# An expert stage in which a product of 512 columns replaces two of 256, and VectorE adds the halves

## The chip, the cores and the metric

The kernel runs on one core of one Trainium2 chip. The metric is its time on the device in microseconds (us), the median of several executions.

## The reference, cut to what matters

A network of two blocks and a third, for 256 tokens of width 1024 in float32. All of it runs in one kernel; the change lies in the last part, a feed-forward layer of 16384 small experts, of which each token picks a few. The kernel computes it densely:

```
act[e, t]   = gelu(sum_d w_down[e, d] * h[t, d])      for all 16384 experts e
out[t, :]  += sum_e gate[e, t] * act[e, t] * w_up[e, :]
```

`gate[e, t]` is zero for nearly all pairs. It is a sum over the picks of token t, each an outer product of two one-hot vectors of length 128 with a weight.

## The kernel before, in words

Each 32-bit weight w is split into a high part, `whi` (w rounded to fp32r), and a low part, `wlo` = w - `whi`; activations likewise (`hhi`, `hlo`, `chi`, `clo`). A product is then three: high x high, high x low and low x high. `pe_mm3` (lines 556 to 573) issues the three.

**Blocks.** SyncE loads slabs of 2048 columns into a ring of 3 (`raw`). A slab is two blocks of 1024 columns. ScalarE makes the high part of a block (line 2400, `cut_hi`), then VectorE or GpSimd the low part (line 1345, `cut_lo`), both into rings of 3 blocks. ScalarE waits until TensorE has used up the block three before. Which engine makes a low part is said by `lo_engine`: in the two earlier feed-forward layers VectorE and GpSimd take turns, of the expert layer's first 12 blocks GpSimd makes all, and VectorE all that follow. `ve_cuts` and `se_cuts` let each engine run two blocks ahead of the block that TensorE is at.

**The expert layer.** The 16384 experts are 128 groups of 128, called "experts" 0 to 127 in the code and here. Expert i has a down block (8 tiles of 128x128) and an up block (1024 columns). Its down block gives `h` times `w_down`, 128 experts x 256 tokens, in one half of a PSUM bank (24 products of 256 columns, `pe_expert_down`); ScalarE applies gelu from PSUM (line 2945); VectorE multiplies with the gates (line 2347), rounds (2352) and subtracts (2354), `ve_weigh`; then 12 products of 512 columns with the up block add into four banks that hold the output (lines 565 to 567).

The order has four stretches:

- down blocks 0 to 20, while VectorE picks the experts of each token;
- down blocks 21 to 71, "where gates are built": between them stand 64 gate steps, one or two behind each of the experts 21 to 68 (`steps`). For a step VectorE makes one-hots for four tokens (four TENSOR_SCALAR, line 2324, and one TENSOR_TENSOR of 512 columns, line 2327), TensorE multiplies them (line 1300), ScalarE copies the result out (line 2959), and DMAs spill it. Results of gelu wait in `ge_t`;
- up blocks 0 to 70 alone;
- from expert 72 (`NST`) on, down and up blocks alternate: down i+1, up i.

PSUM banks go round: all eight where gates are built, four for the down blocks behind.

All is written by hand: each engine has its own list of work (`pe_`, `ve_`, `se_`, `ge_`, and `sync` for the DMAs), and semaphores are counted from it.

## Time and profile before

| | |
|---|---|
| runs | 1988.35 us median of 3 (1988.26 to 1988.54) |
| profiled execution, its own time | 1988.46 us |
| its span, first to last instruction | 1986.7 us |
| TensorE (PE) busy | 1897.9 us, 96% |
| VectorE (DVE) busy | 1384.1 us, 70% |
| ScalarE (ACT) busy | 990.0 us, 50% |
| GpSimd (POOL) busy | 257.1 us, 13% |
| mean granted TensorE clock | 0.989 |

PEld is TensorE's load of weights, which runs beside its products. Busy times are averages over stretches with different limits, so a stretch is read by itself. A product is pipelined: its duration overlaps the next one, and the distance from start to start is its price. The same holds in small for VectorE and ScalarE: an instruction that waits for nothing starts some 0.09 us before the end of the one ahead.

### The profile page before, as it was taken

To read this page: it belongs to the slowest core of one execution; us is meant where nothing else is said; L and a number is where in the kernel's file an instruction comes from. 1 tells how busy PE (TensorE), PEld (TensorE's weight loads), DVE (VectorE), ACT (ScalarE), POOL (GpSimd) and SP (SyncE) were. 2 spreads that over 40 slices of the span, in tenths; PEclk is the share of its full clock that TensorE was granted. 3 is DMA by queue.
4 is the path that set the end of the run, shared out by engine and by line. 5 is a ranking of instruction groups with operands and counts; after the bars stand their busy time and mean duration, and the time that the engine had idled before them with its cause. 6 is when DMAs were issued, how large, how long until landed. Compare 5 with 4: busy or idle time off the path is not lost.

```text
span 1986.7 us, 33458 instructions
## 1 busy us (share of the span) xinstructions
PE 1897.9 (96%) x13306; PEld 1751.9 (88%) x13306; DVE 1384.1 (70%) x2518; ACT 990.0 (50%) x1442; POOL 257.1 (13%) x118
## 2 busy tenths in 40 slices
PE   6989899999988999999999899999999999999998
PEld 6887799999968799999898799999988888999997
DVE  5897775558957773347666559988878887666665
ACT  5645544455435554455555445566653334444444
POOL 0001044440001034430000065000000000000000
PEclk8999999999999999999999999999999999999999
DMA  8754467765564255545434354577766866465452
GB/s 319 245 189 142 150 237 258 258 225 199 183 229 154 97 194 181 188 170 201 166 129 168 111 175 161 184 219 215 219 206 255 301 240 231 179 231 193 174 208 107
DMA packets 94553, 391.96 MB, mean 197 GB/s; under 512 B 7680, under 2 KB 41776, under 8 KB 56000
## 3 DMA queue, kind: packets, MB, share of 16 engines
q1 hardware_dynamic: 94112, 389.58, 56.4%
q8 instruction: 106, 1.74, 0.4%
q14 instruction: 47, 0.39, 0.1%
q10 hardware_dynamic: 288, 0.26, 0.1%
HBM read 371.72 MB, written 15.73 MB: 195 GB/s over the span
## 4 chain that ended last, share of the span: by engine, by line
PE 77%; DVE 11%; ACT 3%; issue 2%; DMA 1%; POOL 0%; ACTq 0%; DVEq 0%; SPq 0%
PE ps L569 10%; PE ps L571 10%; PE ps L570 10%; PE acc L565 9%; PE acc L566 9%; PE acc L567 9%; PE acc L569 3%; PE acc L570 3%; PE acc L571 3%; DVE wlo L1345 2%; PE ps L1300 1%; PE acc L1300 1%; DVE arena L1374 1%; PE ps L1043 1%; PE ps L714 1%
## 5 line engine op out<-in xcount | busy, mean ns | idle before, releaser
L2400 ACT ACTIVATE whi<-raw 128x1024 fp32r<-128x1024 f32 x557 | 588.7, 1060 | 484.7 <-PE acc L567 273.1
L1345 DVE TENSOR_TENSOR wlo<-raw,whi 128x1024 fp32r<-128x1024 f32 x461 | 569.2, 1242 | 292.6 <-ACT whi L2400 289.5
L569 PE MATMUL ps<-hhi,whi 128*128 128x256 f32 x1848 | 527.3, 285 | 7.0 <-DVE wlo L1345 3.1
L571 PE MATMUL ps<-hhi,wlo 128*128 128x256 f32 x1848 | 522.8, 283 | 0.0
L570 PE MATMUL ps<-hlo,whi 128*128 128x256 f32 x1848 | 522.7, 283 | 0.0
L569 PEld LDWEIGHTS ps<-hhi,whi 128*128 128x128 f32 x1848 | 354.1, 192 | 12.9 <-issue 4.1
L570 PEld LDWEIGHTS ps<-hlo,whi 128*128 128x128 f32 x1848 | 354.3, 192 | 2.8
L571 PEld LDWEIGHTS ps<-hhi,wlo 128*128 128x128 f32 x1848 | 354.1, 192 | 0.0
L1345 POOL TENSOR_TENSOR wlo<-raw,whi 128x1024 fp32r<-128x1024 f32 x96 | 239.8, 2501 | 616.6 <-ACT whi L2400 616.4
L565 PE MATMUL acc<-whi,chi 128*128 128x512 f32 x752 | 296.0, 394 | 3.5 <-DVE wlo L1345 1.9
L566 PE MATMUL acc<-whi,clo 128*128 128x512 f32 x752 | 294.5, 392 | 0.0
L567 PE MATMUL acc<-wlo,chi 128*128 128x512 f32 x752 | 293.5, 390 | 0.0
L569 PE MATMUL acc<-hhi,whi 128*128 128x256 f32 x672 | 195.3, 291 | 11.5 <-DVE wlo L1345 4.8
L570 PE MATMUL acc<-hlo,whi 128*128 128x256 f32 x672 | 191.1, 284 | 0.0
L571 PE MATMUL acc<-hhi,wlo 128*128 128x256 f32 x672 | 191.1, 284 | 0.0
L565 PEld LDWEIGHTS acc<-whi,chi 128*128 128x128 f32 x752 | 142.1, 189 | 32.5 <-issue 2.9
L567 PEld LDWEIGHTS acc<-wlo,chi 128*128 128x128 f32 x752 | 141.8, 189 | 30.4
L566 PEld LDWEIGHTS acc<-whi,clo 128*128 128x128 f32 x752 | 142.1, 189 | 26.3
L1374 DVE SCALAR_TENSOR_TENSOR arena<-arena,gs_t 128x512 f32<-128x512 f32 x140 | 130.9, 935 | 24.5 <-DMA arena<-in_ada 15.4
L569 PEld LDWEIGHTS acc<-hhi,whi 128*128 128x128 f32 x672 | 129.9, 193 | 14.5 <-ACT hhi L2514 4.6
L570 PEld LDWEIGHTS acc<-hlo,whi 128*128 128x128 f32 x672 | 130.1, 194 | 0.0
L571 PEld LDWEIGHTS acc<-hhi,wlo 128*128 128x128 f32 x672 | 129.9, 193 | 0.0
(452 smaller groups left out, 2399.7 us busy)
## 6 DMA issues: line engine op xcount, KB each, us to landing
raw<-in_peer_down SPq DMA_DIRECT2D x64, 1024.0 KB, 5.0
raw<-in_peer_up SPq DMA_DIRECT2D x64, 1024.0 KB, 5.0
arena<-in_ada SPq DMA_DIRECT2D x80, 512.0 KB, 5.1
raw<-in_w_gate SPq DMA_DIRECT2D x22, 1024.0 KB, 4.8
raw<-in_w_up SPq DMA_DIRECT2D x22, 1024.0 KB, 4.8
raw<-in_w_down SPq DMA_DIRECT2D x22, 1024.0 KB, 4.8
arena<-spill SPq DMA_DIRECT2D x14, 1024.0 KB, 7.0
spill<-hT_t SPq DMA_DIRECT2D x22, 448.0 KB, 5.9
```

Of the source, the lines that this page charges most:

```text
L565: e.matmul(out, xh, hi, start=start, stop=False, skip_group_check=True)
L566: e.matmul(out, xl, hi, start=False, stop=False, skip_group_check=True)
L567: i = e.matmul(out, xh, lo, start=False, stop=stop, skip_group_check=True)
L569: e.matmul(out, hi, xh, start=start, stop=False, skip_group_check=True)
L570: e.matmul(out, hi, xl, start=False, stop=False, skip_group_check=True)
L571: i = e.matmul(out, lo, xh, start=False, stop=stop, skip_group_check=True)
L714: i = e.matmul(ps[:, j * 128:(j + 1) * 128], self.m.ada_acc[:, j * 128:(j + 1) * 128], self.m.ones, start=True, stop=True, skip_group_chec ...
L1043: t = e.matmul(ps[0:30, 0:256], m.zb[:, 8 * i + k, :], w[:, k, :], start=i == 0 and k == 0, stop=i == 1 and k == 7, skip_group_check=True)
L1300: t = e.matmul(ps[:, i * 128:(i + 1) * 128], m.oh1[:, n % 3, i * 128:(i + 1) * 128], m.oh2[n % 3][:, i * 128:(i + 1) * 128], start=True, s ...
L1345: e.tensor_tensor(out=lo, in0=w, in1=hi.bitcast(F32), op=ALU.subtract).then_inc(*X(("lo", j)))
L1374: e.scalar_tensor_tensor(out=m.ada_acc, in0=w, scalar=c, in1=m.ada_acc, op0=ALU.mult, op1=ALU.add).then_inc(*V(*([("ada", s)] if k else [])))
L2400: e.activation(hi, w, ACT.Copy, scale=1.0).then_inc(*self.A(("hi", j)))
```

## The change

- `hhi` and `hlo` become the halves of one buffer, `hpair`, so that one operand (`hP`) can take the high and the low activations of a tile side by side, 2 x 256 columns.
- From expert 21 (`STEP0`) on a tile of a down block is two products (`pe_mm2`): high weights x 512 columns into the whole bank, and low weights x the 256 high columns into its first half.
- VectorE adds the two halves of the bank with a TENSOR_REDUCE (`ve_halves`) into `ge_t` or `co`; gelu (`se_gelu`) then works in place on SBUF. Experts 0 to 20 keep the old way.
- `lo_engine`: of the down blocks 21 to 71 the second of each slab (experts 21, 23, ... 71) goes to GpSimd.
- Where gates are built, ScalarE copies out the gates of expert i-1's steps and applies its gelu one block later, behind the high part that it cuts for expert i.

```diff
@@ lo_engine
+        if name == "peer_down" and STEP0 <= 2 * i + half < NST:
+            return ("V", "G")[half]
@@ Memory
-        hhi, hlo = sb("hhi", [128, 2048], F32R), sb("hlo", [128, 2048], F32R)
+        hpair = sb("hpair", [128, 4096], F32R)
...
+        self.hP = hpair[:, :].rearrange("p (s a t) -> p a s t", s=2, a=8)
+        self.hH, self.hL, self.cH, self.cL = self.hP[:, :, 0, :], self.hP[:, :, 1, :], tiles8(chi), tiles8(clo)
@@ new
+    def pe_mm2(self, e, ps, tile, k, *keys):
+        hi, lo, end = tile
+        if end is not None:
+            keys = (*keys, ("used", end))
+        e.matmul(ps.rearrange("p (s t) -> p s t", s=2), hi, self.m.hP[:, k], start=k == 0, stop=False, skip_group_check=True)
+        i = e.matmul(ps[:, 0:T], lo, self.m.hH[:, k, :], start=False, stop=k == 7, skip_group_check=True)
...
+    def ve_halves(self, e, dst, *key):
+        src = self.banks.tile(*key)[:, :].rearrange("p (s t) -> p t s", s=2)
+        e.wait_ge(*self.at("full", *key))
+        e.tensor_reduce(out=dst, in_=src, axis=AX, op=ALU.add, negate=False).then_inc(*self.V(("out", *key)))
@@ ve_gates
             self.ve_cuts(e, "peer_down", 8 * i + 7)
+            if i > STEP0:
+                self.ve_expert_halves(e, i - 1)
@@ ve_experts
         self.ve_weigh(e, 0)
+        self.ve_expert_halves(e, NST - 1)
         for i in range(128):
             if i + 1 >= NST and i < 127:
                 self.ve_cuts(e, "peer_down", 8 * (i + 2) - 1)
+            if NST <= i + 1 < 128:
+                self.ve_expert_halves(e, i + 1)
+                self.ve_cuts(e, "peer_up", 8 * (i + 1) - 1)
             if i < 127:
                 self.ve_weigh(e, i + 1)
@@ se_gates
+            self.se_cuts(e, "peer_down", 8 * i + 7)
+            if i > STEP0:
+                for n in steps(i - 1):
+                    self.se_gates_out(e, n)
+                self.se_gelu(e, i - 1)
@@ se_experts
             if i + 1 >= NST and i < 127:
-                self.se_expert_down(e, i + 1)
+                self.se_cuts(e, "peer_down", 8 * (i + 1) + 7)
+                if i + 1 == NST:
+                    self.se_gelu(e, NST - 1)
+                self.se_gelu(e, i + 1)
```

The order of instructions at two places. First VectorE where gates are built; L1345 (before) and L1363 (after) make a low part, the rows with `kc_t` are one-hots (one gate step is a row of L2324 and one of L2327), L1400 adds halves. Before, three experts:

```order
L1345 TENSOR_TENSOR wlo<-raw,whi 128x1024
L2324 TENSOR_SCALAR arena<-kc_t,arena 128x128 x4
L2327 TENSOR_TENSOR arena<-kc_t,arena 128x512
L1345 TENSOR_TENSOR wlo<-raw,whi 128x1024
L2324 TENSOR_SCALAR arena<-kc_t,arena 128x128 x4
L2327 TENSOR_TENSOR rs_t<-kc_t,arena 128x512
L1345 TENSOR_TENSOR wlo<-raw,whi 128x1024
L2324 TENSOR_SCALAR arena<-kc_t,arena 128x128 x4
L2327 TENSOR_TENSOR rs_t<-kc_t,arena 128x512
```

After the change, three experts:

```order
L2351 TENSOR_SCALAR arena<-kc_t,arena 128x128 x4
L2354 TENSOR_TENSOR rs_t<-kc_t,arena 128x512
L1400 TENSOR_REDUCE arena<-acc 128x256
L2351 TENSOR_SCALAR arena<-kc_t,arena 128x128 x4
L2354 TENSOR_TENSOR rs_t<-kc_t,arena 128x512
L2351 TENSOR_SCALAR arena<-kc_t,arena 128x128 x4
L2354 TENSOR_TENSOR arena<-kc_t,arena 128x512
L1363 TENSOR_TENSOR wlo<-raw,whi 128x1024
L1400 TENSOR_REDUCE arena<-ps 128x256
L2351 TENSOR_SCALAR arena<-kc_t,arena 128x128 x4
L2354 TENSOR_TENSOR rs_t<-kc_t,arena 128x512
L1400 TENSOR_REDUCE arena<-ps 128x256
```

What moved: behind each expert's one-hots there is a reduction, and only one expert in two has a low part left on VectorE. The other 26 stand on POOL, in the order of their blocks: it has 88 low parts behind the first feed-forward layer's 34, where it had 62.

Second, VectorE where down and up blocks alternate. One pair before (`x2`: an up block and the next down block):

```order
L2354 TENSOR_TENSOR clo<-rs_t,chi 128x256
L1345 TENSOR_TENSOR wlo<-raw,whi 128x1024 x2
L2347 TENSOR_TENSOR rs_t<-rs_t,arena 128x256
L2352 CAST chi<-rs_t 128x256
L2354 TENSOR_TENSOR clo<-rs_t,chi 128x256
```

and after:

```order
L2388 TENSOR_TENSOR clo<-rs_t,chi 128x256
L1363 TENSOR_TENSOR wlo<-raw,whi 128x1024
L1400 TENSOR_REDUCE rs_t<-ps 128x256
L1363 TENSOR_TENSOR wlo<-raw,whi 128x1024
L2381 TENSOR_TENSOR rs_t<-rs_t,arena 128x256
L2386 CAST chi<-rs_t 128x256
L2388 TENSOR_TENSOR clo<-rs_t,chi 128x256
```

What moved: the two low parts are torn apart. Behind the one of the down block stands the reduction, then the low part of the up block, and then the weighing (`rs_t`, CAST, `clo`), which stood ahead of it. On ACT the order is as before, gelu and then two high parts, but gelu now waits for the reduction.

## Rows read from the trace of the kernel before

**Rows 1.** The page: the span, and the busy time of PE.
```profile
span 1986.7 us, 33458 instructions
...
PE 1897.9 (96%) x13306; PEld 1751.9 (88%) x13306; DVE 1384.1 (70%) x2518; ACT 990.0 (50%) x1442; POOL 257.1 (13%) x118
```

**Rows 2.** Busy time per stretch: start:end, its length, each engine (instructions), clock, DMA share, GB/s.
```profile
1264.00:1460.00 196.00, 196.00 (x1672) 195.97 (x1671) 160.97 (x365) 131.22 (x161) 0.00 (x0) 1.00 0.72 213
...
1470.00:1660.00 190.00, 190.00 (x840) 157.39 (x839) 159.28 (x279) 74.27 (x70) 0.00 (x0) 1.00 0.69 249
...
1664.00:1960.00 296.00, 296.00 (x1898) 270.10 (x1897) 184.90 (x265) 126.24 (x158) 0.00 (x0) 1.00 0.54 200
```

**Rows 3.** Order of time, PE, one pair: start us, duration us, engine, line, operation.
```profile
1812.05 0.28 PE L569 MATMUL ps<-hhi,whi 128*128 128x256 f32 x1
...
1814.92 0.40 PE L565 MATMUL acc<-whi,chi 128*128 128x512 f32 x1
...
1817.67 0.28 PE L569 MATMUL ps<-hhi,whi 128*128 128x256 f32 x1
```

**Rows 4.** The same view, PE, where gates are built: the first product of two down blocks.
```profile
1383.42 0.37 PE L569 MATMUL acc<-hhi,whi 128*128 128x256 f32 x1
...
1395.62 0.37 PE L569 MATMUL acc<-hhi,whi 128*128 128x256 f32 x1
```

**Rows 5.** The same view, DVE, where gates are built.
```profile
1380.09 1.11 DVE L2324 TENSOR_SCALAR arena<-kc_t,arena 128x128 f32<-128x128 f32 x4
...
1381.12 0.68 DVE L2327 TENSOR_TENSOR rs_t<-kc_t,arena 128x512 f32<-128x512 f32 x1
...
1381.72 1.22 DVE L1345 TENSOR_TENSOR wlo<-raw,whi 128x1024 fp32r<-128x1024 f32 x1
...
1382.85 1.11 DVE L2324 TENSOR_SCALAR arena<-kc_t,arena 128x128 f32<-128x128 f32 x4
...
1385.82 1.23 DVE L1345 TENSOR_TENSOR wlo<-raw,whi 128x1024 fp32r<-128x1024 f32 x1 [1.25 <-ACT whi L2400]
```

**Rows 6.** The same view, DVE and POOL in the first FFN; then the view of line 1371.
```profile
262.45 1.54 DVE L1374 SCALAR_TENSOR_TENSOR arena<-arena,gs_t 128x512 f32<-128x512 f32 x2
...
265.23 3.50 DVE L1374 SCALAR_TENSOR_TENSOR arena<-arena,gs_t 128x512 f32<-128x512 f32 x2
...
264.16 3.23 POOL L1345 TENSOR_TENSOR wlo<-raw,whi 128x1024 fp32r<-128x1024 f32 x1 [3.00 <-ACT whi L2400]
...
L1371 DVE TENSOR_SCALAR arena<-arena,gs_t x20: 444/478/2573, 45.7 to 707.3; 128x512 f32<-128x512 f32 x20
```

**Rows 7.** Groups of DVE instructions by line and shape: busy us, mean ns.
```profile
L2324 DVE TENSOR_SCALAR arena<-kc_t,arena 128x128 f32<-128x128 f32 x256 | 71.1, 341 | 0.0
...
L1553 DVE TENSOR_REDUCE small<-arena 128x2 f32<-128x512 f32 x20 | 13.7, 686 | 0.7
...
L1575 DVE COPY arena<-ps 128x512 f32<-128x512 f32 x12 | 7.9, 687 | 6.1 <-PE ps L744 5.8
...
L1567 DVE TENSOR_SCALAR arena<-arena,small 128x256 f32<-128x256 f32 x40 | 12.3, 351 | 0.7
```

**Rows 8.** Order of time, DVE and ACT, one pair.
```profile
1815.54 0.43 DVE L2347 TENSOR_TENSOR rs_t<-rs_t,arena 128x256 f32<-128x256 f32 x1 [0.91 <-ACT rs_t L2945]
...
1816.67 1.22 DVE L1345 TENSOR_TENSOR wlo<-raw,whi 128x1024 fp32r<-128x1024 f32 x1
...
1815.12 0.38 ACT L2945 ACTIVATE rs_t<-ps 128x256 f32<-128x256 f32 x1 [1.75 <-PE ps L571]
...
1815.40 1.05 ACT L2400 ACTIVATE whi<-raw 128x1024 fp32r<-128x1024 f32 x1
```

**Rows 9.** The same view, PE, from the last down product of the gates' stretch.
```profile
1465.26 0.28 PE L571 MATMUL ps<-hhi,wlo 128*128 128x256 f32 x1
...
1467.10 0.47 PE L565 MATMUL acc<-whi,chi 128*128 128x512 f32 x1 [1.56 <-DVE clo L2354]
```

More of the change, by code:

```diff
@@ L300, in tiles8 @@
             return ap[:, :].rearrange("p (a t) -> p a t", a=8)
-        self.hH, self.hL, self.cH, self.cL = tiles8(hhi), tiles8(hlo), tiles8(chi), tiles8(clo)
+        self.hP = hpair[:, :].rearrange("p (s a t) -> p a s t", s=2, a=8)
+        self.hH, self.hL, self.cH, self.cL = self.hP[:, :, 0, :], self.hP[:, :, 1, :], tiles8(chi), tiles8(clo)
         self.hT = tiles8(self.hT_t)
@@ L571, in pe_mm3 @@
             i = e.matmul(out, lo, xh, start=False, stop=stop, skip_group_check=True)
+        if keys:
+            i.then_inc(*self.P(*keys))
+    def pe_mm2(self, e, ps, tile, k, *keys):
[4 more added lines that the diff above has]
+        i = e.matmul(ps[:, 0:T], lo, self.m.hH[:, k, :], start=False, stop=k == 7, skip_group_check=True)
         if keys:
@@ L1268, in pe_expert_down @@
         ps = self.banks.take(e, "expert", i)
+        if i >= STEP0:
+            for k in range(8):
+                self.pe_mm2(e, ps, self.W.tile(e, "peer_down", 8 * i + k), k, *([("full", "expert", i)] if k == 7 else []))
+            return
         for k in range(8):
@@ L2329, in ve_one_hots, with ve_expert_halves @@
                             *V(("oh2", n)))
+    def ve_expert_halves(self, e, i):
+        m = self.m
+        if i >= NST + 2:
+            e.wait_ge(*self.at("weighed", i - 2))
+        self.ve_halves(e, m.ge_t[i] if i < NST else m.co[:, i % 2, :], "expert", i)
     def ve_weigh(self, e, i):
@@ L2336, in ve_weigh @@
         w = m.co[:, 2 + s, :]
-        e.wait_ge(*self.at("out", "expert", i))
+        e.wait_ge(*self.at("gelu", i))
         if i == 0:
@@ L2940, in se_expert_down, with se_gelu, se_gates_out @@
         e.wait_ge(*self.at("full", "expert", i))
-        if i >= NST + 2:
-            e.wait_ge(*self.at("weighed", i - 2))
-        elif i == NPRE + 16:
-            e.wait_ge(*self.at("end", "picked", "P"))
-        e.activation(m.ge_t[i] if i < NST else m.co[:, i % 2, :], self.banks.tile("expert", i)[:, 0:T],
-                     ACT.Gelu_apprx_tanh, scale=1.0).then_inc(*self.A(("out", "expert", i)))
+        e.activation(m.ge_t[i], self.banks.tile("expert", i)[:, 0:T], ACT.Gelu_apprx_tanh, scale=1.0).then_inc(
+            *self.A(("out", "expert", i), ("gelu", i)))
+    def se_gelu(self, e, i):
+        x = self.m.ge_t[i] if i < NST else self.m.co[:, i % 2, :]
+        e.wait_ge(*self.at("out", "expert", i))
+        e.activation(x, x, ACT.Gelu_apprx_tanh, scale=1.0).then_inc(*self.A(("gelu", i)))
     def se_gates(self, e):
-        m, A = self.m, self.A
         for i in range(STEP0, NST):
-            self.se_expert_down(e, i)
-            for n in steps(i):
-                k, c = n // 2 % 3, n // 6
-                st = m.stage[k].rearrange("p (n t) -> p n t", t=8)[:, :, 4 * (n % 2):4 * (n % 2) + 4]
-                e.wait_ge(*self.at("full", "gates", n))
-                if c and n % 2 == 0:
-                    e.wait_ge(self.spilled[k], 16 * c)
-                    e.wait_ge(self.kept, 16 * (n // 2 - 2))
-                e.activation(st.rearrange("p n t -> p t n"), self.banks.tile("gates", n)[:, :].rearrange(
-                    "p (t n) -> p t n", t=4), ACT.Copy, scale=1.0).then_inc(*A(("out", "gates", n)))
+            self.se_cuts(e, "peer_down", 8 * i + 7)
[3 more added lines that the diff above has]
+                self.se_gelu(e, i - 1)
+    def se_gates_out(self, e, n):
+        m = self.m
+        k, c = n // 2 % 3, n // 6
+        st = m.stage[k].rearrange("p (n t) -> p n t", t=8)[:, :, 4 * (n % 2):4 * (n % 2) + 4]
+        e.wait_ge(*self.at("full", "gates", n))
+        if c and n % 2 == 0:
+            e.wait_ge(self.spilled[k], 16 * c)
+            e.wait_ge(self.kept, 16 * (n // 2 - 2))
+        e.activation(st.rearrange("p n t -> p t n"), self.banks.tile("gates", n)[:, :].rearrange("p (t n) -> p t n", t=4),
+                     ACT.Copy, scale=1.0).then_inc(*self.A(("out", "gates", n)))
     def se_experts(self, e):
```

## The prediction

> The time for a change is worked out against the profiled execution: span 1986.7 us, its own time 1988.46 us, which is 0.1 us over the median of the runs shown, 1988.35. What the change adds to or takes from the span is added to that median. About 0.2%, 4 us, is what a measurement of this kernel can tell from no change.
>
> **What bounds the kernel now.** First the page: PE is busy 1897.9 of 1986.7 us [rows 1]. Then the stretches that the change touches, taken alone: where gates are built (1264 to 1460), where up products run alone (1470 to 1660) and where down and up products alternate (1664 to 1960), PE is busy for all of 196, 190 and 296 us, at a granted clock of 1.00, while DVE is busy for 161, 159 and 185 [rows 2]. Busy time does not say at which pace, so the next view is the order of time on PE. In the alternating stretch a down block, 24 products of 256 columns, takes 1812.05 to 1814.92, 0.1196 us each, and an up block, 12 products of 512 columns, 1814.92 to 1817.67, 0.229 us each; then the next down block follows with no gap [rows 3]. The durations of 0.28 and 0.40 in these rows overlap each other; the steps from start to start are what counts. Where gates are built, three experts with their four gate steps take 1383.42 to 1395.62, 12.20 us [rows 4]. So PE alone sets both paces: 12.20 us for three experts, and 2.87 + 2.75 = 5.62 us for a pair of blocks.
>
> **1. Products of 512 columns.** A tile now costs 0.229 + 0.120 = 0.349 us where it was 3 x 0.1196 = 0.359. The same columns stream; only one start is saved. Per expert 8 x 0.010 = 0.08 us, 2.79 where it was 2.87. For 107 experts (21 to 127) that is 8.6 us at most: 4.1 in the 51 experts of the gates' stretch, 4.5 in the 56 behind. The moving operand is now two pieces of 256 columns, which no row shows. The bounds are one product of 512 (0.229) and two of 256 (0.239, which would give nothing back); I take the first. One weight load less changes nothing, since loads lie beside products.
>
> **2. The halves added on DVE.** 107 new TENSOR_REDUCE from 512 elements in PSUM to 256. Nearest rows: a reduce from 128x512 takes 686 ns, a COPY of 512 from PSUM 687 [rows 7], so I take 0.69 us, or 0.60 from start to start behind another (a 0.68 us one-hot product is followed after 0.60 [rows 5]). None of the rows has 256 outputs; from below one of 0.60, from above two passes, 1.3. Gelu moves behind it and reads SBUF: 0.38 us from PSUM [rows 8], at most 0.05 more.
>
> The Trainium skill (VectorE: DVE Perf Modes, the TRN2 errata) counts 62 cycles more for a PSUM source than for SBUF. That would be 0.75 us here and a total of +11, an estimate from that page; the equal 686 and 687 speak against it.
>
> **3. Half the low parts to GpSimd.** 26 blocks (experts 21, 23 to 71) leave DVE, 1.13 us each from start to start [rows 5], and cost GpSimd some 2.4. GpSimd is otherwise empty there, and PE needs a block two experts after the one whose buffer it takes is used, some 8.1 us [rows 4]; that covers 1.06 + 2.4. What is not covered is DVE. In the trace DVE stands still while GpSimd subtracts: two SCALAR_TENSOR_TENSOR take 1.54 us with GpSimd idle and 3.50 while GpSimd runs from 264.16 to 267.39, which is itself stretched to 3.23 by DVE's subtraction before [rows 6]. That is 1.96 us lost per GpSimd operation. A TENSOR_SCALAR of 128x512 whose median is 478 ns took up to 2573 [rows 6], so one-input operations from SBUF are caught too. It runs at double pace: from 256 columns (351 ns [rows 7]) to 512 it needs 0.127 us more, where one column per clock from PSUM needs 0.69 for 512. The one-hots of L2324 are of that kind (341 ns with two scalars) and will be caught. Operations from PSUM, which no row shows beside GpSimd, I take to be free of it.
>
> By the Trainium skill (SBUF, Who interferes with whom) the pair of ports is an exclusive lock, taken by operations with two SBUF inputs and by fast one-input modes, never by tensor_reduce. The trace agrees, by rows 6, for the first two.
>
> **4. The sum where gates are built**, per six experts (eight gate steps, three low parts on each engine). PE: 24.40 before, 24.40 - 6 x 0.08 = 23.92 now. DVE: a step is 1.03 + 0.60 = 1.63 [rows 5], eight are 13.04; three low parts 3.39; six reductions 3.60; together 20.03, about what it was (13.04 + 6.78 = 19.82). To this come three stalls. Full stalls of 2.03 (1.96 and a little wait for the handover) less a reduction running under each would be 1.43; the middle, 1.73, gives 5.19. Sum 25.2. DVE then sets the pace, 0.8 over the old 24.40. Over the 48 experts with steps: 8 x 0.82 = **+6.6 us**. Who waits: PE's gate steps, for one-hots. Bounds: all stalls hidden, PE at 23.92, -4; three whole operations of 2.4, 27.2, +22.
>
> **5. End of the gates' stretch.** Before, PE pauses from the last down product at 1465.26 to 1467.10, for DVE's first weighing [rows 9]. Now DVE has halves of expert 70 and its backlog in front of it: 0.6 to 1.2, **+1 us** taken.
>
> **6. First pair.** Gelu of expert 71 stands on ACT behind the high part of down block 73, which waits until PE has used up block 70. From there 1.05 + 0.4 (gelu) + 1.13 (weighing) + 1.2 (low part of up block 71) with hand-overs is 4.0 us, against 2.79 of down block 72: **+1.2**, and some 0.6 until the chain has settled: **+1.8**.
>
> **7. The alternating stretch.** PE now needs 2.79 + 2.75 = 5.54 us for a pair. DVE and ACT form a ring: halves (0.69), gelu (0.28 to 0.33 until the next ACT start), high part 1.05, low part of the up block 1.13, weighing 1.13 (1815.54 to 1816.67), low part of the down block 1.13, next halves; with two hand-overs of 0.03 to 0.04 that is 5.48 to 5.53 [rows 5, 7, 8]. Before, the low part of the up block stood behind the weighing and nothing closed the ring. It is as long as PE's own 5.54, so PE keeps the pace by a hair: 56 x 0.08 = **-4.5 us**. Each 0.1 us more in the reduction would cost 5.6.
>
> The 71 up blocks alone are unchanged. SP's order is unchanged too: slabs wait for the same low parts, and three ring slots cover a GpSimd block's 1.3 us more. The wait for the bank (now freed by DVE) has eight banks behind it. Sum: 6.6 + 1.0 + 1.8 - 4.5 = +4.9, so 1993.3 us.
>
> **Rivals.**
> A, *the stalls are hidden and PE keeps both paces*. For it: DVE was idle for 35 of 196 us [rows 2], and a GpSimd block may fall on waits and reductions. It decides if a GpSimd operation costs DVE under (23.92 - 20.03) / 3 = 1.3 us. Then -4.1 + 0.5 + 1.8 - 4.5 = -6.3: 1982.0. Against it: DVE's idle time came from waits for high parts in front of low parts, and these are the halves that GpSimd now makes.
> B, *the reduction is dearer*, since it writes 256 results, or the split moving operand gives nothing. At 0.9 us DVE's ring is 5.72, +0.10 x 56 = +5.6 in place of -4.5; the gates' stretch gets 8 x 6 x 0.2 = +9.6 more: +24.6, 2013. At 0.75: some 1998.
> C, *whole GpSimd operations fall on DVE*: 2.4 each, +22 in place of +6.6: 2009.
> That halves or GpSimd blocks are not there is excluded by the order of the instructions.
>
> **Chances.** Forecast 0.50 (+1 to +12; of it 0.14 within 4 us), A 0.23 (nearly all below -4, 0.03 within), B 0.16, C 0.11. Faster 0.20, same 0.17, slower 0.63. The range leaves out the dearest of B and the far end of A: 1980 to 2009.
>
> **What would show it.** In the gates' stretch DVE near 100% busy, with one-hots of over 2 us beside each GpSimd low part; PE no longer full, waiting for DVE's one-hots; about 202 us for what took 196. The new reduction at 0.69. Down blocks of 2.79 on PE. In the alternating stretch a period of 5.54 to 5.56, and DVE's halves starting right behind its low part. I am wrong if PE stays full where gates are built (A), if the reduction is over 0.8 us or a 512-column product over 0.235 (B).

## The result, and the profile after

The changed kernel takes **1998.3 us** (median of 6 runs, 1995.91 to 2004.54), the kernel before on the same chips 1987.8 us (6 runs). The ratio is 1.0061, 95% interval 1.0048 to 1.0073: slower by 10.5 us as a difference of the medians, by 12 as the ratio has it. 1993.3 us was forecast, a change of +4.9. The direction is right and the main cause is right; the change came out 5.6 us dearer.

The profiled execution of the changed kernel took 2004.54 us, 6 us over its median. 3.7 us of its distance to the profile before arise ahead of everything that the change touches (the last COPY_PREDICATED of the expert choice starts at 1257.63 where it was 1253.94); the granted clock from 600 to 660 us was 0.89 there and 0.95 in the profile before, and 0.91 against 1.00 from 900 to 920. What follows therefore goes by the length of stages, not by the span.

The page of the changed kernel: span, busy time, and the chain that ended last by engine and by line.

```profile
span 2002.7 us, 31852 instructions
...
PE 1899.2 (95%) x12450; PEld 1709.7 (85%) x12450; DVE 1455.8 (73%) x2599; ACT 992.5 (50%) x1442; POOL 319.9 (16%) x144
...
PE 68%; DVE 21%; ACT 3%; issue 2%; DMA 1%; POOL 0%; ACTq 0%; DVEq 0%; SPq 0%
```

PE is as busy as before [rows 1] although it has fewer products, and DVE now has 21% of the chain, where it had 11%. The windows of the changed kernel (start:end, length, then PE, PEld, DVE, ACT, POOL busy, clock, DMA share, GB/s): first to last gate step, six microseconds just behind the first up product, and the stretch in which down and up blocks alternate.

```profile
1273.20:1470.60 197.40, 190.60 (x1263) 172.59 (x1264) 197.40 (x387) 127.09 (x155) 55.47 (x23) 1.00 0.67 204
1482.00:1488.00 6.00, 6.00 (x21) 4.73 (x20) 4.22 (x8) 1.06 (x1) 0.00 (x0) 0.72 0.28 119
1664.00:1960.00 296.00, 294.81 (x1469) 247.15 (x1468) 212.98 (x318) 127.04 (x157) 0.00 (x0) 1.00 0.52 199
```

Against [rows 2]: where gates are built DVE is busy for all of 197.40 us and PE no longer is. Before, the same piece of work, first to last gate step, was this window, 192.4 us long, with PE full and DVE at 159.8:

```profile
1264.20:1456.60 192.40, 192.40 (x1641) 192.39 (x1640) 159.79 (x363) 128.66 (x158) 0.00 (x0) 1.00 0.71 211
```

The reason stands in the order of time of DVE where gates are built, changed kernel.

```profile
1378.58 3.22 DVE L2351 TENSOR_SCALAR arena<-kc_t,arena 128x128 f32<-128x128 f32 x4
1381.72 0.68 DVE L2354 TENSOR_TENSOR arena<-kc_t,arena 128x512 f32<-128x512 f32 x1
1382.33 0.68 DVE L1400 TENSOR_REDUCE arena<-ps 128x256 f32<-128x512 f32 x1
1382.93 1.10 DVE L2351 TENSOR_SCALAR arena<-kc_t,arena 128x128 f32<-128x128 f32 x4
...
1387.91 0.68 DVE L1400 TENSOR_REDUCE arena<-ps 128x256 f32<-128x512 f32 x1
1388.52 2.60 DVE L2351 TENSOR_SCALAR arena<-kc_t,arena 128x128 f32<-128x128 f32 x4
```

The same for GpSimd.

```profile
1378.56 2.40 POOL L1363 TENSOR_TENSOR wlo<-raw,whi 128x1024 fp32r<-128x1024 f32 x1 [4.71 <-ACT whi L2438]
1387.84 2.42 POOL L1363 TENSOR_TENSOR wlo<-raw,whi 128x1024 fp32r<-128x1024 f32 x1 [6.89 <-ACT whi L2438]
```

Four one-hots take 1.10 us with GpSimd idle, and 3.22 where its subtraction starts with them. At 1387.84 it starts 0.07 us ahead of a reduction; the reduction takes its usual 0.68 us and only the one-hots behind it are held, 2.60 us. Of the 24 GpSimd blocks that meet one-hots, 15 begin ahead of a reduction like this one and hold the one-hots for 1.5 us; the other nine hold them for 1.9 to 2.2. Over the whole stretch the mean of a one-hot rose from 341 ns [rows 7] to 496:

```profile
L2351 DVE TENSOR_SCALAR arena<-kc_t,arena 128x128 f32<-128x128 f32 x256 | 111.8, 496 | 0.0
```

The 256 of them took 111.8 us where they took 71.1 [rows 7]. That is 1.7 us for each of the 24; of the other two GpSimd blocks, one runs beside the expert choice and one behind the last gate step.

The reduction itself: the view of its line in the changed kernel (ns as min/median/max), and who waited for it.

```profile
L1400 DVE TENSOR_REDUCE rs_t<-ps x56: 682/684/693, 1681.4 to 1988.8; 128x256 f32<-128x512 f32 x56
L1400 DVE TENSOR_REDUCE arena<-ps x27: 671/680/684, 1275.8 to 1481.2; 128x256 f32<-128x512 f32 x27
...
  ACT rs_t L2986: 142.3, 56
```

Two stalls stand at the start of the gates' stretch. PE's waits from 1250 to 1480 in the changed kernel (total us, times, longest):

```profile
PE ps L1318 <- DVE rs_t L2354: 4.6, 4, 1.8
PE acc L572 <- DVE wlo L1363: 3.4, 3, 2.5
PE acc L1318 <- DVE arena L2354: 1.8, 2, 0.9
PE acc L1318 <- DVE rs_t L2354: 1.3, 2, 0.9
PE ps L1318 <- DVE arena L2354: 0.8, 1, 0.8
```

Before, the longest wait for a low part in this place was 0.6 us. What DVE did there, changed kernel; GpSimd's first two blocks run from 1258.61 and from 1269.26:

```profile
1257.63 4.51 DVE L2277 COPY_PREDICATED arena<-arena 128x256 f32<-128x256 uint32 x2
...
1269.52 2.99 DVE L2351 TENSOR_SCALAR arena<-kc_t,arena 128x128 f32<-128x128 f32 x4
```

The two COPY_PREDICATED took 2.61 us before. DVE's next low part is 1.9 us later for it, and PE waits for that. The first one-hots are held as well, so from the last of the picked transposes (six products that turn the picked experts' numbers round for the gate steps) to the first gate step it is 4.9 us instead of 3.0.

Last, PE in the alternating stretch of the changed kernel: the first pair's stall, and later one down block from its first product to that of the up block, and the next down block.

```profile
1680.52 0.47 PE L568 MATMUL acc<-whi,chi 128*128 128x512 f32 x1 [1.18 <-DVE wlo L1363]
...
1683.36 0.39 PE L584 MATMUL ps<-hpair,whi 128*128 128x512 f32 x1
1683.59 0.28 PE L585 MATMUL ps<-hpair,wlo 128*128 128x256 f32 x1
...
1686.17 0.40 PE L568 MATMUL acc<-whi,chi 128*128 128x512 f32 x1
...
1688.96 0.39 PE L584 MATMUL ps<-hpair,whi 128*128 128x512 f32 x1
```

Down block 2.81 us, up block 2.79: a period of 5.60 us, where it was 5.62 [rows 3] and 5.54 was forecast.

The pace where gates are built is best read over equal pieces of work. Eight gate steps and six experts took 24.40 us before [rows 4]. In the changed kernel, from one gate step to the one 24 steps later, PE takes 75.32 us, 25.11 for eight:

```profile
1322.92 1.05 PE L1318 MATMUL acc<-rs_t,arena 128*128 128x128 f32 x8
...
1398.24 1.05 PE L1318 MATMUL ps<-rs_t,arena 128*128 128x128 f32 x8
```

Table of stages, each measured on PE in the profiled execution (us), from start to start. "To first step" runs from the last of the picked transposes to the first gate step; "gate steps" from there to the last product of the last step, which takes in all 64 steps and the 47 down blocks between them; "to up" from the first product of the last step to the first up product; "pairs" from the first down product of expert 72 to the last `whi`, `chi` product of expert 127.

| kernel | to first step | gate steps | to up | 71 up blocks | pairs |
|---|---|---|---|---|---|
| before | 3.0 | 192.4 | 11.25 | 193.2 | 317.7 |
| changed | 4.9 | 197.4 | 11.7 | 194.8 | 317.9 |
| all low parts on DVE | 3.0 | 188.7 | 11.5 | 193.2 | 317.8 |
| GpSimd blocks alone | 5.0 | 193.9 | 11.25 | 193.2 | 317.7 |
| GpSimd blocks cut short | 3.0 | 188.7 | 11.5 | 193.2 | 318.0 |
| halves side by side | 5.0 | 197.8 | 11.7 | 194.9 | 317.9 |
| all on DVE, other orders | 3.0 | 188.7 | 11.5 | 193.2 | 316.2 |
| pairs only | 3.0 | 192.4 | 11.25 | 193.2 | 316.2 |
| GpSimd from expert 27 | 3.0 | 197.4 | 11.7 | 193.2 | 317.9 |
| no halves among pairs | 3.0 | 188.7 | 11.5 | 193.2 | 317.6 |
| 512 first, then 256 | 3.0 | 188.8 | 11.5 | 194.9 | 311.9 |
| a fourth on GpSimd | 3.0 | 192.1 | 11.6 | 193.2 | 317.8 |

### The profile page after: what moved, and what is told of

Same layout as the page of the kernel before. It is cut to its first block, busy times and chain, and to the rows that moved or that the text cites. A ratio compares the mean times of both kernels' runs of the same rounds, so it can differ in the third digit from the quotient of the medians.

```text
span 2002.7 us, 31852 instructions
## 1 busy us (share of the span) xinstructions
PE 1899.2 (95%) x12450; PEld 1709.7 (85%) x12450; DVE 1455.8 (73%) x2599; ACT 992.5 (50%) x1442; POOL 319.9 (16%) x144
## 4 chain that ended last, share of the span: by engine, by line
PE 68%; DVE 21%; ACT 3%; issue 2%; DMA 1%; POOL 0%; ACTq 0%; DVEq 0%; SPq 0%
PE acc L568 9%; PE acc L570 9%; PE acc L569 9%; PE ps L572 6%; PE ps L574 6%; PE ps L573 6%; PE ps L584 5%; DVE arena L2351 5%; DVE wlo L1363 3%; PE ps L585 3%; PE acc L572 2%; PE acc L573 2%; PE acc L574 2%; DVE arena L1400 1%; DVE arena L1392 1%
## 5 line engine op out<-in xcount | busy, mean ns | idle before, releaser
L1363 DVE TENSOR_TENSOR wlo<-raw,whi 128x1024 fp32r<-128x1024 f32 x435 | 537.1, 1242 | 280.1 <-ACT whi L2438 279.6
L1363 POOL TENSOR_TENSOR wlo<-raw,whi 128x1024 fp32r<-128x1024 f32 x122 | 302.5, 2482 | 800.4 <-ACT whi L2438 800.2
L572 PE MATMUL ps<-hpair,whi 128*128 128x256 f32 x1184 | 337.7, 285 | 7.0 <-DVE wlo L1363 3.1
L573 PE MATMUL ps<-hpair,whi 128*128 128x256 f32 x1184 | 335.0, 283 | 0.0
L574 PE MATMUL ps<-hpair,wlo 128*128 128x256 f32 x1184 | 334.9, 283 | 0.0
L584 PE MATMUL ps<-hpair,whi 128*128 128x512 f32 x664 | 238.8, 400 | 0.0
L572 PEld LDWEIGHTS ps<-hpair,whi 128*128 128x128 f32 x1184 | 226.9, 192 | 10.8 <-issue 4.1
L573 PEld LDWEIGHTS ps<-hpair,whi 128*128 128x128 f32 x1184 | 227.1, 192 | 0.6
L574 PEld LDWEIGHTS ps<-hpair,wlo 128*128 128x128 f32 x1184 | 227.0, 192 | 0.0
L585 PE MATMUL ps<-hpair,wlo 128*128 128x256 f32 x664 | 186.1, 280 | 0.0
L572 PE MATMUL acc<-hpair,whi 128*128 128x256 f32 x480 | 140.3, 292 | 15.0 <-DVE wlo L1363 8.3
L584 PEld LDWEIGHTS ps<-hpair,whi 128*128 128x128 f32 x664 | 124.8, 188 | 28.7
L573 PE MATMUL acc<-hpair,whi 128*128 128x256 f32 x480 | 138.2, 288 | 0.0
L574 PE MATMUL acc<-hpair,wlo 128*128 128x256 f32 x480 | 138.1, 288 | 0.0
```

Source lines behind the costliest of these rows:

```text
L572: e.matmul(out, hi, xh, start=start, stop=False, skip_group_check=True)
L573: e.matmul(out, hi, xl, start=False, stop=False, skip_group_check=True)
L574: i = e.matmul(out, lo, xh, start=False, stop=stop, skip_group_check=True)
L584: e.matmul(ps.rearrange("p (s t) -> p s t", s=2), hi, self.m.hP[:, k], start=k == 0, stop=False, skip_group_check=True)
L585: i = e.matmul(ps[:, 0:T], lo, self.m.hH[:, k, :], start=False, stop=k == 7, skip_group_check=True)
L1363: e.tensor_tensor(out=lo, in0=w, in1=hi.bitcast(F32), op=ALU.subtract).then_inc(*X(("lo", j)))
```

## The experiments

My theory after reading the two traces: GpSimd's subtraction holds up DVE instructions beside it, DVE becomes the bound where gates are built, and that costs more than the 512-column products earn. The rivals: the reductions do it, or the later gates, or the memory layout of the moving operand.

### All low parts on DVE

```
         if name[:6] in ("w_gate", "w_up0", "w_up1", "w_down"):
             return ("V", "G")[j % 2]
-        if name == "peer_down" and STEP0 <= 2 * i + half < NST:
-            return ("V", "G")[half]
```

> The changed kernel without the two lines in lo_engine: VectorE makes all low parts where gates are built, GpSimd none. My theory (VectorE loses about 2 us under each of the 26 GpSimd operations): VectorE's own work per six experts rises from 20.0 to 13.04 + 6 x 1.13 + 6 x 0.60 = 23.4 us, but nothing stalls it, and PE needs 24.40 - 6 x 0.06 = 24.0 with the down block of 2.81 us measured after the change. So PE sets the pace again: from the first to the last gate step 185 to 187 us (187.8 before, 196.6 after the change), and a total of 1985 to 1989. Rival (the reductions overload VectorE, whoever makes the low parts): with 3.4 us more of its own per six experts the stretch is as long as after the change or longer, 196 to 203, and the total 1998 to 2006.

Measured: 1980.97 us, ratio to before 0.9976 (0.9964 to 0.9987): **faster than before**, by 0.24%. The window of its gate steps:

```profile
1259.80:1448.50 188.70, 188.70 (x1267) 172.03 (x1265) 186.10 (x410) 132.92 (x157) 0.00 (x0) 1.00 0.70 215
```

PE is full again and DVE, which now makes 23 low parts more in this stretch, is busy for 11 us less than in the changed kernel: each GpSimd block had cost DVE (197.4 - 186.1) / 23 = 0.49 us more than it took off. The work handed to GpSimd was worth more on DVE than off it. The gates' stretch is 3.7 us shorter than before, and both stalls at its start are gone. Without its GpSimd blocks the change would have been a gain. PE's own pace, 24 gate steps apart, is 71.80 us, 23.93 for eight:

```profile
1307.74 1.05 PE L1316 MATMUL acc<-rs_t,arena 128*128 128x128 f32 x8
...
1379.54 1.05 PE L1316 MATMUL ps<-rs_t,arena 128*128 128x128 f32 x8
```

The whole came out 4 us under the lower end of what I had put down; on these chips the kernel before took 1984.8 us, 3 less than on those of the result. The 187.8 and 196.6 us in the expectation were counted from other borders than the table's 192.4 and 197.4.

### GpSimd blocks alone

The kernel before with the two lines of `lo_engine` added and nothing else.

```
+        if name == "peer_down" and STEP0 <= 2 * i + half < NST:
+            return ("V", "G")[half]
```

> The kernel before with only the two lines in lo_engine added: GpSimd makes 26 low parts, products and gelu as before. My theory: each GpSimd operation stalls VectorE by 1.7 to 2.0 us, but VectorE has 13.04 + 3.39 + 3 x 1.9 = 22.1 us per six experts against PE's 24.4, so PE keeps the pace: 187.8 to 189 us from the first to the last gate step, total 1988 to 1990. VectorE's busy time in the stretch rises all the same, from 161 us in 196 to about 175. Rival (PE waits for low parts that GpSimd makes late): the stretch is 190 to 197 us, and PE's waits name POOL's low part.

Measured: 1994.72 us, ratio 1.0039 (1.0023 to 1.0054). The window of its gate steps:

```profile
1270.50:1464.40 193.90, 193.90 (x1641) 193.90 (x1641) 162.28 (x339) 128.52 (x157) 65.49 (x23) 0.99 0.70 209
```

The two COPY_PREDICATED in its order of DVE:

```profile
1254.80 4.50 DVE L2254 COPY_PREDICATED arena<-arena 128x256 f32<-128x256 uint32 x2
```

Here DVE has no reductions, so it has room: 162.28 of 193.90 us, and PE is never without work. The steps cost 1.5 us more than before, and all of that lies in the first eight of them (26.0 us for 24.5; each eight behind take 24.41 as before). There the granted clock was 0.50 for a while, behind PE's waits at the start:

```profile
1272.00:1275.00 3.00, 3.00 (x16) 3.00 (x15) 1.33 (x3) 1.65 (x2) 0.00 (x0) 0.50 0.38 158
```

So in the even part of the stretch GpSimd's blocks cost this kernel nothing. The two stalls at the start are the same as in the changed kernel, 4.50 for 2.61 and 5.0 for 3.0. So they belong to GpSimd's first blocks alone. The whole came out over what I had put down, as I had counted the steps and not the start. DVE's busy time had been expected at about 175 us in 196 and stayed at 162: only 16 of the 26 blocks held one-hots.

### GpSimd blocks cut short

The changed kernel, but GpSimd's operation covers 64 of 1024 columns. The other 960 low parts of those blocks are left out of the result.

```
                 e.wait_ge(*self.at("hi", j))
+                if who == "G" and self.W.blocks[j][0] == "peer_down" and STEP0 <= 2 * self.W.blocks[j][1] + self.W.blocks[j][2]:
+                    w, hi, lo = w[:, 0:64], hi[:, 0:64], lo[:, 0:64]
```

> The changed kernel with the 26 operations of GpSimd cut from 1024 to 64 columns (of these low parts 960 of 1024 columns are left out, so what TensorE reads there is old); VectorE's instructions, their order and every wait are the same. My theory: with some 0.3 us in place of 2.4 per operation VectorE's stalls nearly vanish, and its own 20.0 us per six experts lie far under PE's 24.0: 185 to 186 us from the first to the last gate step, total 1985 to 1989. Rival (the work or the order of the reductions sets the pace): 196 us as after the change, total 1998, since none of that is touched.

Measured: 1982.87 us, ratio 0.9989 (0.9978 to 1.0000).

```profile
1262.30:1451.00 188.70, 188.70 (x1265) 171.99 (x1264) 161.58 (x387) 133.27 (x158) 8.99 (x24) 1.00 0.67 213
```

Order, waits and counts of instructions are those of the changed kernel; only the time in which GpSimd works is taken away, 55 us to 9. DVE falls from 197.4 to 161.6 us and PE is full. What slowed DVE is the overlap itself, not the waits that come with another engine. The steps took 188.7 us where 185 to 186 had been put down, by the other borders named above, and the whole came out 2 us under its range.

### Halves side by side

The high and low halves of one k stand next to each other in memory, so a 512-column product reads 512 words in a row instead of two pieces of 256.

```
-        self.hP = hpair[:, :].rearrange("p (s a t) -> p a s t", s=2, a=8)
+        self.hP = hpair[:, :].rearrange("p (a s t) -> p a s t", s=2, a=8)
```

> The changed kernel with hpair laid out by tiles, so that the 512 columns of the moving operand lie together (2 KB) and not in two pieces 8 KB apart. Theory a (the split operand costs 0.006 us per product, 0.235 from start to start where 0.229 was measured before): down blocks of 2.77 to 2.79 us in place of 2.81, pairs of 5.56 to 5.57, total 1 to 2 us less than the changed kernel. Theory b (the pitch comes from the alternation of 512 and 256 columns, not from the operand): 2.81 and 5.595 as after the change, total unchanged at 1998.

Measured: 1999.63 us, ratio 1.0058 (1.0042 to 1.0073); pairs 317.9 us. No stage differs from the changed kernel by more than 0.4 us, and the 0.4 is in the gate steps, where this execution had a second stretch at a granted clock of 0.50 (1279 to 1282). The split operand is not what makes a down block 2.81 us.

### All on DVE, weighing first, gelu of expert 71 earlier

```
                 self.ve_expert_halves(e, i + 1)
-                self.ve_cuts(e, "peer_up", 8 * (i + 1) - 1)
             if i < 127:
                 self.ve_weigh(e, i + 1)
...
                 self.se_gelu(e, i - 1)
+        self.se_gelu(e, NST - 1)
...
                 self.se_cuts(e, "peer_down", 8 * (i + 1) + 7)
-                if i + 1 == NST:
-                    self.se_gelu(e, NST - 1)
```

and the two lines of `lo_engine` taken out.

> The change without its GpSimd blocks (all low parts on DVE), and two orders altered: DVE weighs an expert right behind its halves, with the low part of the up block after the weighing instead of before it, and ACT does the gelu of expert 71 at the end of the gates' loop, ahead of the high part of down block 73. Theory A (a ring of DVE and ACT sets the pairs' period of 5.60 us: halves, gelu, high part of the up block, its low part, weighing, low part of the down block, halves, all back to back in the trace): the new order opens the ring, so the pairs' period falls to PE's own, 5.54 us or less, and the pairs' stage takes 313 to 315 us instead of 317.83; the stall of 1.2 us behind the first down block of the pairs is gone as well. Whole: about 1977 us beside 1981 for the version with all low parts on DVE, ratio to before 0.995 to 0.997. Theory B (PE's own pitch of 0.232 to 0.235 us for the products beside 512-column ones sets 5.60): the stage falls only by the 1.2 us of the first stall, to 316.6 us, and the whole is about 1979.8 us, ratio 0.997. The gates' steps take 188.7 us either way.

Measured: 1981.07 us, ratio 0.9968 (0.9955 to 0.9981), pairs 316.17 us. The order of DVE in one of its pairs:

```profile
1864.26 1.23 DVE L1361 TENSOR_TENSOR wlo<-raw,whi 128x1024 fp32r<-128x1024 f32 x1 [0.35 <-ACT whi L2435]
1865.99 0.69 DVE L1398 TENSOR_REDUCE rs_t<-ps 128x256 f32<-128x512 f32 x1 [0.50 <-PE ps L583]
```

The ring is open, for DVE now waits 0.50 us for PE ahead of each reduction. Yet the period is 5.60 us, as it was. Theory A falls: DVE and ACT did not set it. The 1.66 us that the stage lost are the stall of the first pair. The whole fits theory B (ratio 0.997), not A.

### Pairs only

The kernel before with `pe_mm2` and the halves from expert 72 on; gates' stretch as before, no GpSimd blocks, gelu of expert 71 from PSUM in its old place.

```
-        if i >= STEP0:
+        if i >= NST:
             for k in range(8):
```

> The kernel before, with the products of 512 columns and the halves from expert 72 on only (gates' stretch as before, no GpSimd low parts). Both theories: the gates' steps take 192.4 us as before and the 71 up blocks 193.2 us. Pairs' stage 317.8 us as in the change (317.66 before), since either the ring or the pitch holds it; so the whole is the time of before, ratio 0.999 to 1.001: the 512-column products earn nothing among the pairs, and the 3.8 us that the all-DVE version gained all come from the gates' stretch. If the ratio were below 0.998, that would be wrong.

Measured: 1986.68 us, ratio 0.9994 (0.9985 to 1.0003), no difference. Its pairs take 316.17 us, 1.6 less than I had put down: there is no first stall, and 512-column products in this order earn 1.5 us over 56 pairs. DVE's order within a pair is that of the changed kernel here, so the old place of expert 71's gelu is enough to take the first stall away.

### GpSimd from expert 27 on

```
-        if name == "peer_down" and STEP0 <= 2 * i + half < NST:
+        if name == "peer_down" and STEP0 + 6 <= 2 * i + half < NST:
```

> The change with GpSimd's low parts from expert 27 on instead of from 21 (23 blocks instead of 26). Theory: the two stalls at the start of the gates' stretch (low part behind the slowed COPY_PREDICATED, +1.9 us; first one-hots, +2.1 us) belong to the first blocks on GpSimd and go: the wait of PE for the last low part of the route is 0.6 us again, and from the last picked transpose to the first gate step 3.6 us instead of 5.7. The gates' steps keep most of their 197.4 us, since DVE is still caught by the others: about 196.5 us (three blocks of 26 fewer, 8.7 us times 3/26 = 1 us less). Whole about 5 us under the change: 1993 us beside 1998, ratio to before 1.003 to 1.004. Rival: the two stalls come from the products of 512 columns or from the later gates, and stay; then the whole is within 1.5 us of the change, ratio 1.005 to 1.006.

Measured: 1993.41 us, ratio 1.0039 (1.0025 to 1.0053). Both stalls at the start are gone: the longest wait for a low part of the expert choice is 0.6 us, and the first gate step comes 3.0 us behind the picked transposes (the expectation's 3.6 and 5.7 count from an earlier product). Its interval is clear of the one with all low parts on DVE, so the rest of the loss is still there:

```profile
1261.90:1459.30 197.40, 190.30 (x1264) 172.44 (x1264) 197.40 (x389) 128.13 (x156) 53.04 (x22) 1.00 0.67 205
```

The steps take 197.4 us where I expected 196.5. I had counted three blocks fewer, but two of the three start ahead of the first gate step: the window holds 22 in place of 23. At 0.49 a block, 22 give 186.1 + 10.8 = 196.9; that even this half microsecond does not show stays open. The whole is 0.22% under the changed kernel. The two intervals overlap a little, but the vanished stalls stand in the trace, so some 4 us of the loss arise at the start of the stretch and the rest inside it.

### A fourth of the low parts on GpSimd

```
-        if name == "peer_down" and STEP0 <= 2 * i + half < NST:
-            return ("V", "G")[half]
+        if name == "peer_down" and STEP0 + 6 <= 2 * i + half < NST:
+            return ("V", "G")[half * (i % 2)]
```

> The change with GpSimd making only every fourth down block's low part from expert 27 on: 12 blocks instead of 26. Theory (each GpSimd block takes 1.22 us of its own off DVE and adds some 1.7 us to the DVE instructions beside it, so it costs DVE 0.47 us, and the gates' steps take the larger of PE's 188.7 us and DVE's 186.1 + 0.47 a block): DVE's sum is 186.1 + 12 x 0.47 = 191.7 us, steps 190.5 to 192.5 us, no stalls at the start, whole some 3 us over the version with all on DVE, ratio to before 0.998 to 1.000. Rival (one block in four finds cover, since DVE has 2.6 us free in the steps and PE has a queue ahead): steps 188.7 us, ratio 0.997.

Measured: 1985.91 us, ratio 1.0000 (0.9988 to 1.0012).

```profile
1260.10:1452.20 192.10, 189.60 (x1266) 172.31 (x1265) 192.10 (x400) 130.70 (x157) 26.87 (x11) 1.00 0.70 211
```

With 11 blocks in the window the steps take 192.1 us, with 23 of them 197.4, with none 188.7 (PE's, over 186.1 of DVE). At 0.49 a block 11 would give 191.5. The number of blocks sets the time once DVE's sum is over PE's. The rival, that one block in four finds cover, falls.

### No halves among the pairs

All low parts on DVE; from expert 72 on the addition is left out and gelu is taken from the first half in PSUM. The products with the low part of h are missing from the result of those experts.

```
+        if key[1] >= NST:
+            return
         src = self.banks.tile(*key)[:, :].rearrange("p (s t) -> p t s", s=2)
```

> All low parts on DVE, and from expert 72 on the addition of the halves is left out: ACT takes the gelu from the first half in PSUM alone, so the second half (the products with the low part of h) is missing from the result of those experts. Everything else as in the version with all low parts on DVE (pairs 317.83 us). Theory A (the ring of DVE and ACT sets the period): without its 0.73 us the ring is under 4.9 us, so the period falls to PE's own, 5.54 us or less; pairs' stage 313 to 315 us. Theory B (PE's own pitch beside 512-column products): the stage stays within 1.5 us of 317.8 us. The gates' steps take 188.7 us.

Measured: 1984.38 us, ratio 0.9986 (0.9976 to 0.9997), pairs 317.6 us. Three rows of PE:

```profile
1864.93 0.39 PE L582 MATMUL ps<-hpair,whi 128*128 128x512 f32 x1
...
1867.74 0.40 PE L566 MATMUL acc<-whi,chi 128*128 128x512 f32 x1
...
1870.53 0.39 PE L582 MATMUL ps<-hpair,whi 128*128 128x512 f32 x1
```

2.81 + 2.79 again, with 0.7 us less for DVE in each pair and no reader of the bank but ACT. The period is PE's own, as theory B has it.

### First the products of 512, then those of 256

The version with the other orders, and in each down block the eight products of 512 columns first, then the eight of 256.

```
-            for k in range(8):
-                self.pe_mm2(e, ps, self.W.tile(e, "peer_down", 8 * i + k), k, *([("full", "expert", i)] if k == 7 else []))
+            los = []
+            for k in range(8):
+                hi, lo, end = self.W.tile(e, "peer_down", 8 * i + k)
+                e.matmul(ps.rearrange("p (s t) -> p s t", s=2), hi, m.hP[:, k], start=k == 0, stop=False, skip_group_check=True)
+                los.append((lo, end))
+            for k, (lo, end) in enumerate(los):
+                keys = ([("used", end)] if end is not None else []) + ([("full", "expert", i)] if k == 7 else [])
+                i2 = e.matmul(ps[:, 0:T], lo, m.hH[:, k, :], start=False, stop=k == 7, skip_group_check=True)
+                if keys:
+                    i2.then_inc(*self.P(*keys))
```

> The version with all low parts on DVE, the weighing ahead of the up block's low part and the early gelu of expert 71 (pairs' stage 316.17 us, period 5.595 us, gates' steps 188.7 us, whole 0.9968 of before), and in each down block from expert 21 on the eight products of 512 columns first and then the eight of 256, where they alternated. Theory P (a product of 512 columns costs 0.235 us to the next start because a 256-column product stands beside it): eight in a row go at 0.227 as they do in the up blocks alone, a down block takes 8 x 0.227 + 8 x 0.12 = 2.77 us instead of 2.81 and the pairs' period is 5.53 to 5.56, stage 312.5 to 314.5 us. Theory Q (the pitch of 0.232 to 0.235 goes with the stretch, whatever the neighbour): the period stays 5.59 to 5.60, the stage 316.2 us, and the whole is equal to the version that alternates, ratio 0.9965 to 0.997.

Measured: **1976.81 us**, ratio 0.9943 (0.9926 to 0.9959): 10 us under the kernel before and the fastest of all versions. PE in one pair of it:

```profile
1865.12 1.98 PE L1285 MATMUL ps<-hpair,whi 128*128 128x512 f32 x8
1866.93 1.11 PE L1289 MATMUL ps<-hpair,wlo 128*128 128x256 f32 x8
1867.88 0.40 PE L566 MATMUL acc<-whi,chi 128*128 128x512 f32 x1
...
1870.63 1.98 PE L1285 MATMUL ps<-hpair,whi 128*128 128x512 f32 x8
```

Eight products of 512 in 1.81 us are 0.226 each, eight of 256 in 0.95 are 0.119; the down block takes 2.76 and the up block 2.75, as before the change. The period is 5.51 us and the pairs' stage 311.9 us. Theory P holds among the pairs, and the stage came out a little under what it said. Where gates are built nothing was gained: 188.8 us. The eight of 512 take 1390.04 to 1391.97, 0.241 each:

```profile
1390.04 2.10 PE L1285 MATMUL acc<-hpair,whi 128*128 128x512 f32 x8
1391.97 1.11 PE L1289 MATMUL acc<-hpair,wlo 128*128 128x256 f32 x8
```

The first product behind a gate step is the dear one there, 0.32 us to the next start (a first product of 256 took 0.20 before); the other seven take 0.232 each, where among the pairs they take 0.227. A down block of the gates' stretch takes 2.88 us in either order, where it took 2.96.

## Why the prediction was right or wrong

**What sets the pace where gates are built (term 4): right, in its parts too.** +6.6 us was forecast, +5.0 measured. DVE is busy for 100% of the stretch, one-hots take 2.6 to 3.3 us beside each GpSimd block, and PE's gate steps wait for one-hots. Taking away GpSimd's working time alone takes away the loss. Per six experts, 24.40 us before, 23.92 for PE alone and 25.2 for DVE were put down; 24.41, 23.93 and 25.11 are measured. DVE's own work of 20.03 leaves 5.08 for three GpSimd blocks, 1.69 each: two of three meet a reduction first and cost 1.5, the third 2.1, so the "middle" of 1.73 was near for a reason, though the prediction gave none. This is 0.56 a block more than the 1.13 of a low part; 0.49 is the mean over the whole window. Rival C, 2.4, is out, and rival A would have needed under 1.3. The forecast's surplus of 1.6 us is, about half and half, the 0.1 us per six experts by which DVE's pace was put too high, and the first eight steps, which took only 0.1 us more than before (24.6 for 24.5).

The Trainium skill (SBUF — State Buffer, Who interferes with whom) has the shared ports as an exclusive lock that a reduction never needs. This trace agrees: 0.68 us for the reduction that runs under GpSimd, up to 3.22 us for four one-hots of 1.10.

**Term 1 in that stretch: right.** 0.08 us per expert was forecast for PE; a down block fell from 2.96 to 2.88, and with all low parts on DVE the 47 blocks in the window gave the 3.7 us back.

**The start of the gates' stretch: the missing term.** Term 3 said that a GpSimd block is covered and the prediction looked only at the steady order of six experts. The first block falls on COPY_PREDICATED at the end of the expert choice (+1.9 us), where PE has no queue of work to live on, and the second on the very first one-hots (+1.9). GpSimd from expert 27 on removes both, and the whole falls from 1.0061 to 1.0039 of before. Behind these stalls TensorE's granted clock was 0.50 for a while in the profiled execution, which is the 1.2 GHz level:

```profile
1266.00:1268.00 2.00, 2.00 (x11) 2.00 (x11) 0.00 (x0) 0.15 (x1) 0.00 (x0) 0.50 0.64 270
```

The picked transposes began 6.9 us later than before; 3.7 were there ahead of them and 1.9 are the stall, so 1.3 are left for the clock, and 0.2 more pass within the transposes themselves. The same two stalls with a granted clock of 0.50 behind them stand in the three profiled executions that have GpSimd's first blocks (changed, halves side by side, GpSimd blocks alone), and in none of the other nine. This term of 3.8 us, put at nothing, is the larger of two that make the sum too small; the other is the saving among the pairs.

**The reduction (term 2): right.** 679 to 687 ns against 0.69 forecast, and no dearer for writing 256 results. Rival B's first half, 0.75 or 0.9 us, falls. The Trainium skill (VectorE: DVE Perf Modes, the TRN2 errata) counts more cycles for a PSUM source, 0.75 us by the prediction's estimate from it; this trace speaks against it.

**End of the stretch (term 5)**: +1 forecast, +0.5 measured. **First pair (term 6)**: the first down block and its stall take 4.15 us in place of 2.81, +1.3, where +1.2 and 0.6 of settling were forecast. The cause is confirmed: where the gelu stands ahead of the high part, the stage is 1.7 us shorter (all on DVE with other orders, and pairs only).

**The alternating stretch (terms 1 and 7): the mechanism right, the size wrong.** The term that was mis-sized is the saving of 0.08 us a pair: 56 x 0.08 = -4.5 us was forecast, -1.5 measured in the kernel that has nothing else (pairs only). I took 0.229 + 0.120 for a tile, prices read where a product stands among its like. In alternation a tile takes 0.351, of it 0.235 for the product of 512, the very limit that the prediction had named as a sign against it; the up products behind such a block take 0.232 instead of 0.229, so a pair saves 0.025 us instead of 0.08. The price of one kind of product depended on what stood around it: with products of one kind together, the pairs' stage is 4.3 us shorter (316.2 to 311.9). I had weighed a split operand as the doubtful point; it is without effect. I had also seen DVE's ring as long as PE's period and said that PE keeps the pace by a hair; that PE and not the ring keeps it is shown by two runs, with the ring opened and with 0.7 us taken out of it.

**"The 71 up blocks alone are unchanged"**: in the profile they take 1.6 us more, all of it at their start. Products stand 0.43 us apart there instead of 0.23, which is the 1.2 GHz level of the clock:

```profile
1483.38 0.63 PE L569 MATMUL acc<-whi,clo 128*128 128x512 f32 x1
1483.81 0.63 PE L570 MATMUL acc<-wlo,chi 128*128 128x512 f32 x1
```

It follows PE's wait of 2.18 us for the first weighing, which was 1.56 us before [rows 9]. The three kernels that wait 1.56 us keep their clock; of the nine that wait 2.0 to 2.3 us three lose it: the version with GpSimd from expert 27 waits 2.28 us and keeps it, and the one with 512 first, without GpSimd, loses it. So the change made the wait longer, and whether the clock then fell differed from one kernel's profiled execution to the next.

The terms with their measured sizes: 5.0 + 0.5 + 0.25 (pairs, stall and saving together) + 3.8 (start) = 9.5 us; 1.5 and 1.6 us of lowered clock come on top in the profiled execution. The measured difference of the medians is 10.5 us. Against the forecast the start adds 3.8 us and the pairs 3.0 (+0.25 for -2.7), while the gates' stretch and its end take off 2.1. That the sum came within 6 us is in part luck: the misses partly cancel.

## What to carry to other kernels

Before handing VectorE's work to an idle GpSimd, set what GpSimd's operation holds up on VectorE against what it takes off: here 1.7 us against 1.13, and a kernel that would have been 0.24% faster became 0.61% slower. Where DVE had room, in the kernel with the GpSimd blocks alone, the same blocks cost nothing once the start was over. Look at the first instance of a moved piece of work as closely as at the steady state, since its neighbours there are others. Start-to-start prices of products hold only in the order in which they were read; among the pairs products of one width were cheaper together, where gates are built they were not.

## What was not expected of the hardware

- **Products of 512 and 256 columns in turn cost more than eight of one and then eight of the other, among the pairs.** In turn: 0.351 us for one of each. Eight and eight: 0.226 + 0.119 = 0.345, and the 512-column products of the following block fall from 0.232 to 0.229 as well. Moving operand in one piece or two, an extra DVE reader of PSUM or none, made no difference. Why it is so stays open: the width and the place in the bank (all of it or its first half) change together in these orders, and no run parts them. High and low weights in turn, without a change of width, stood in the order before, at 0.12 us for each product of 256. Open too is why the grouping gives nothing where gate steps stand between the blocks; there the 512-column products take 0.232 even in a row.
- **COPY_PREDICATED is held by GpSimd too**: 4.50 us for two of 128x256 that take 2.61, in three kernels (changed, GpSimd blocks alone, halves side by side).
- **GpSimd's operation is itself longer beside the product of one-hots, and that product is not held.** 23 blocks take 65.5 us in the kernel with the GpSimd blocks alone and 55.5 in the changed kernel, where GpSimd starts when the product is nearly over. With the two starting together, the product (two inputs from SBUF) keeps its 0.68 us and GpSimd takes 2.99 instead of 2.40:

```profile
1287.50 0.68 DVE L2329 TENSOR_TENSOR rs_t<-kc_t,arena 128x512 f32<-128x512 f32 x1
...
1287.45 2.99 POOL L1347 TENSOR_TENSOR wlo<-raw,whi 128x1024 fp32r<-128x1024 f32 x1 [5.43 <-ACT whi L2402]
```

- **A stand-still of PE of 2 us is followed by half the clock in some kernels and not in others.** Waits of 2.0 to 2.3 us in the same place had it in three profiled executions (changed, halves side by side, 512 first) and not in six. No run here tells what decides it.
